# Decay-level products of a gated linear attention as 32- and 64-wide blocks: packing, small masks, and a spread by ScalarE

## The chip, the cores and the metric

The kernel runs on one core of one Trainium2 chip. The metric is the device time of one execution in microseconds (us). The kernel before takes 1532.53 us, the median of three runs (1532.47 to 1537.33).

## The reference, cut to what matters

The program is a block of two models in a row, for 256 tokens of width 1024: a first block (two gated feed-forward layers around an LRU, a local attention and a memory attention), then two layers (`LAYERS`) of a token mix and a mixture of experts. The change concerns one part of the token mix, the gated linear attention called hgrn2, with 4 heads of 128 key and 128 value features and chunks of 64 tokens:

```python
b = jnp.cumsum(gb, axis=2)
rel = b[:, :, :, None, :] - b[:, :, None, :, :]
decay = jnp.exp(jnp.where(causal, rel, -jnp.inf))
attn = jnp.einsum('bhtd,bhtsd,bhsd->bhts', qb, decay, kb)
intra = jnp.einsum('bhts,bhsv->bhtv', attn, vb)
```

Between chunks a state carries the same decay on, so that the whole is one causal attention matrix for each head whose entry (t, s) is the sum over d of q[t,d] exp(b[t,d] - b[s,d]) k[s,d].

## The kernel before, in words

The factor exp(b[t] - b[s]) can't be split into a factor of t and one of s over the whole sequence without leaving the range of float32. The kernel splits it by levels. `LEVELS` is 1, 2, 4, ..., 128. At level L the sequence is cut into pairs of blocks of L tokens. With b at the end of the left block as the origin, the right block's queries are scaled by exp(b - origin) and the left block's keys by exp(origin - b); both are written into one tile `hy` (queries in the odd blocks, keys in the even ones). The product of `hy` with itself over the 128 features then holds the attention of the pair (left keys, right queries), and also much that isn't wanted. The diagonal is a product of its own, of the plain keys `hk` and queries `hq`.

The loop `for n in range(8)` on TensorE makes product n (n = 0 the diagonal, n >= 1 the level `LEVELS[n - 1]`) for each of the two 128-token halves `t` and each of 4 heads `h`: 8 products with 128 stationary and 128 moving columns in float32, into `bank[4]` and `bank[5]` (L2055). A last product (L2067) couples the two halves. On VectorE `add_level` takes each product out of its bank: n = 0 by a multiplication with the diagonal mask (L2911), n >= 1 by a `copy_predicated` under the mask of the level, from `level_mask[:, n - 1]` (L2913); each time two instructions of 512 columns, into `attT`, which holds the transposed attention matrix. GpSimd builds `level_mask` (8 masks of 128 columns) near the start of the program (L724 to L740).

Around these products lies other work, in a fixed order for each engine. A round n is on TensorE: the projection `gates{n}` for n >= 1 (L1422: 48 instructions of 256 moving columns, whose weights have been split into two parts by ScalarE, L874, and VectorE, L2320), the product n (L2055), and one step `mla(n)` of a second attention (L1997 transposes, L2005 scores, L2037 transposes). On VectorE: `span(n + 1)` (L2884 and, for the last levels, L2888 and L2896 to L2900), `add_level(n)`, the two multiplications that write `hy` (L2932, L2933), a split of a weight tile (L2320), and from n = 4 the mask, the maxima and the scaling of the second attention (L2942, L2948, L2582, L2583, L2957, L2959). On ScalarE: `gate_out(n)` (L1249), the two exponentials of level n (L1280, L1281), a split (L874), and from n = 4 the exponentials of the second attention (L1302). Product n waits for `hy` of round n - 1; `hy` of round n waits for the exponentials of level n and stands behind `add_level(n)` on VectorE.

After the rounds come `second_pT` (L2011), the values (L2076 to L2079 and L2088, L2090), a normalisation on VectorE (L2972 to L2988, with the low part of `ymT`, L2983), the branch and output projections (L1445), and the mixture of experts.

Of the kernel before, what the change touches and what calls it, by code (L numbers as in the profile page):

```python
# [35 lines left out]
HGH, DK = 4, 128  # L36
# [4 lines left out]
CHUNK = 64  # L41
FB = 256
RING = 6
TILE = 2048
LEVELS = [1, 2, 4, 8, 16, 32, 64, 128]
NEG = -1.0e30
MISC = QL + KVL + ROPE
# [29 lines left out]
def build(nc, a):  # L77

    ctx = ExitStack()
    with ctx:  # L80
# [9 lines left out]
        x = sb("x", [P, T, D])  # L90
# [121 lines left out]
        hy = view(10240, HGH * SEQ)  # L212
        attT = view(11264, 3, HGH, P)
        p_first = view(19008, MH, P)
        p_second = view(16960, MH, SEQ)
# [198 lines left out]
        s = Signals()  # L414
# [247 lines left out]
        def _(pool):  # L662
            done = [0]

            def link(ins):
                done[0] += 1
                ins.then_inc(s["pool_chain"], 1)
                pool.wait_ge(s["pool_chain"], done[0])
# [53 lines left out]
            for p, of_count in ((1, NE - 2), (2, NE - 5), (3, n_wide), (13, NE - 4), (14, n_wide + n_half - 1), (15, NE - 3)):  # L722
                pool.memset(ranks[:, 2, p:p + 1], float(of_count))
            pool.memset(level_mask[:, 0:7, :], 0.0)  # L724
            link(pool.memset(chunk_seg[:, :], 1.0))
            pool.memset(chunk_seg[:, :].rearrange("p (m c) -> p m c", c=CHUNK)[:, :, 0:1], 0.0)
            upper = []
            for n, L in enumerate(LEVELS[:-1]):
                upper.append(level_mask[:, n, :].rearrange("p (m two c) -> p m two c", two=2, c=L)[:, :, 1, :])
                ins = pool.memset(upper[n], 1.0)  # L730
            link(ins)
            for n, L in enumerate(LEVELS[:-1]):
                ins = pool.affine_select(out=upper[n], in_=upper[n], compare_op=ALU.is_ge, fill=0.0,
                                         base=0, pattern=[[-2 * L, P // (2 * L)], [0, L]], channel_multiplier=1)
            link(ins)
            for n, L in enumerate(LEVELS[:-1]):
                pool.affine_select(out=upper[n], in_=upper[n], compare_op=ALU.is_ge, fill=0.0,
                                   base=L - 1, pattern=[[2 * L, P // (2 * L)], [0, L]], channel_multiplier=-1)
            link(pool.memset(level_mask[:, 7, :], 0.0))
            pool.affine_select(out=level_mask[:, 7, :], in_=level_mask[:, 7, :], compare_op=ALU.not_equal, fill=1.0,  # L740
                               base=0, pattern=[[-1, P]], channel_multiplier=1).then_inc(s["patterns"], 1)
            for l in range(LAYERS):

                pool.wait_ge(s["x"], 16 + 8 * l)
                pool.iota(slot_row, [[1, PICKS]], base=1, channel_multiplier=0, allow_small_or_imprecise_dtypes=True)
                pool.iota(slot_col[:, 0:1], [[0, 1]], base=0, channel_multiplier=1, allow_small_or_imprecise_dtypes=True)
                pool.memset(xg[:, :, 2 * SEQ:PICKS], 0.0)
                pool.memset(key[:, 0:1], -1.0)
                pool.memset(key[:, 1:2], -0.5)
                link(pool.memset(before, 1.0))  # L750
                pool.affine_select(out=before, in_=before, compare_op=ALU.is_ge, fill=0.0, base=-1,
                                   pattern=[[1, P]], channel_multiplier=-1).then_inc(s["slot_patterns"], 1)
# [8 lines left out]
        def _(act):  # L761
# [440 lines left out]
            for l in range(LAYERS):  # L1202
# [65 lines left out]
                for n, L in enumerate(LEVELS):  # L1268
# [13 lines left out]
                    if n < 6:  # L1282
                        split(tiles[13 + n])
                    elif n == 7:
                        split(f"br_b0.{l}", after=f"gates6.{l}")
# [66 lines left out]
        def _(pe):  # L1352
# [594 lines left out]
            for l in range(LAYERS):  # L1947
# [14 lines left out]
                by_token(f"proj5.{l}", bank[7], hT_lo_l)  # L1962
                pe.wait_ge(s["h_act"], 3 * l + 1)
                by_token(f"misc0.{l}", bank[0], hT_lo_l)
                by_token(f"misc1.{l}", bank[1], hT_lo_l)
                pe.wait_ge(s["h_act"], 3 * l + 2)
                by_token(f"misc2.{l}", bank[2], hT_lo_l)
# [8 lines left out]
                pe.wait_ge(s["cT_out"], 2 * l + 1)  # L1976
                pe.wait_ge(s["h_act"], 3 * l + 3)
                pe.wait_ge(s["h_dve"], 3 * l + 3)
# [61 lines left out]
                for n in range(8):  # L2040
                    if n >= 3:
                        pe.wait_ge(s["gates"], 8 * l + n - 2)
                    if n:
                        by_token(f"gates{n}.{l}", bank[n % 3], hT_lo_l)
                    if n == 0:
                        pe.wait_ge(s["h_dve"], 3 * l + 2)
                        pe.wait_ge(s["h_act"], 3 * l + 1)
# [15 lines left out]
                pe.wait_ge(s["hy"], 8 * l + 8)  # L2063
                pe.wait_ge(s["level_added"], 9 * l + 8)
                y = hy[:, :].rearrange("p (h s) -> p h s", h=HGH)
# [75 lines left out]
                pe.wait_ge(s["member"], 2 * run - 1)  # L2141
                pe.wait_ge(s["slot_patterns"], run)
                member = rt[:, 14, :]
# [33 lines left out]
        def _(v):  # L2177
            done = [0]

            def link(ins):  # L2180

                done[0] += 1
                ins.then_inc(s["dve_chain"], 1)
                v.wait_ge(s["dve_chain"], done[0])
# [609 lines left out]
            for l in range(LAYERS):  # L2794
# [14 lines left out]

                v.wait_ge(s["h_act"], 3 * l + 3)  # L2810
                for h in range(HGH):
# [63 lines left out]
                v.wait_ge(s["hg"], run)  # L2875
                v.wait_ge(s["h_act"], 3 * l + 1)
                g_flat = hg[:, :, :].rearrange("p h s -> p (h s)")
# [24 lines left out]

                def add_level(n, mask):

                    v.wait_ge(s["level"], 9 * l + n + 1)
                    m = level_mask[:, mask, :].unsqueeze(1).broadcast_to([P, HGH, P])
                    here = level_mask[:, mask, :].bitcast(I32).unsqueeze(1).broadcast_to([P, HGH, P])
# [12 lines left out]
                for n, L in enumerate(LEVELS):  # L2920
                    if n + 1 < len(LEVELS):
                        span(n + 1, LEVELS[n + 1])
                    if n:
                        v.wait_ge(s["level"], 9 * l + n + 1)
                        add_level(n, n - 1)
                    else:
                        add_level(0, 7)
                    v.wait_ge(s["decay"], 8 * l + n + 1)
# [62 lines left out]
                split(f"w_out0.{l}")  # L2991
                v.wait_ge(s["h_act"], 3 * l + 2)
                v.wait_ge(s["oaT"], run)
# [51 lines left out]
                v.wait_ge(s["scores"], run)  # L3045
                v.wait_ge(s["slot_patterns"], run)

# [135 lines left out]
```

## Time and profile before

| what | value |
|---|---|
| median of three runs | 1532.53 us (1532.47 to 1537.33) |
| the profiled execution | span 1534.2 us (the profile gives no other time for it) |
| TensorE busy, its share of the span | 1406.9 us, 92% |
| VectorE busy | 910.0 us, 59% |
| ScalarE busy | 646.6 us, 42% |
| GpSimd busy | 43.6 us, 3% |
| mean granted TensorE clock | 0.966 |

Busy time of an engine is the union of its instructions. The span is from the first to the last instruction of the core. The two runs of the rounds lie from 620 to 700 us (layer 0) and from 1125 to 1205 us (layer 1).

### The profile page before, as it was taken

How to read it: one execution, taken by the hardware profiler on the slowest of the kernel's cores; microseconds unless marked ns; L12 is line 12 of the kernel's file. 1: busy time of each engine (PE TensorE's matmuls, PEld its weight loads, DVE VectorE, ACT ScalarE, POOL GpSimd, SP SyncE). 2: the span in 40 equal slices, each digit the busy share in tenths (PEclk: the TensorE clock that was granted, in tenths of full speed). 3: DMA queues.
4: the chain of work that ended last, by engine and by line, in shares of the span. 5: the costliest groups of instructions: out<-in, count | busy, mean ns of one | idle time of the engine just before them, and what ended most of it. 6: DMA issues, size and time to landing. Idle time of an engine off the chain costs nothing.

```text
span 1534.2 us, 27016 instructions
## 1 busy us (share of the span) xinstructions
PE 1406.9 (92%) x10772; PEld 1135.5 (74%) x10772; DVE 910.0 (59%) x1458; ACT 646.6 (42%) x1044; POOL 43.6 (3%) x105
## 2 busy tenths in 40 slices
PE   6999999999999899998889999969999888999994
PEld 6999979669999797897645666649879764566662
DVE  5978868748788844789550443244477966054323
ACT  5444446644434543554222544234444522244322
POOL 3300000000000000000010000000000001000000
PEclk9999999999999999999889999979999998999998
DMA  9899874357999654432549999995443264999995
GB/s 321 281 337 345 317 238 147 111 187 249 331 347 334 222 153 151 131 119 86 217 183 363 417 418 418 416 335 165 141 138 110 88 242 175 362 416 419 417 417 222
DMA packets 159802, 402.09 MB, mean 262 GB/s; under 512 B 6410, under 2 KB 102396, under 8 KB 143324
## 3 DMA queue, kind: packets, MB, share of 16 engines
q1 hardware_dynamic: 158768, 398.81, 70.9%
q8 instruction: 67, 1.10, 0.3%
q10 hardware_dynamic: 380, 1.08, 0.3%
q0 software_dynamic: 560, 0.88, 0.2%
q14 instruction: 27, 0.22, 0.0%
HBM read 399.70 MB, written 1.05 MB: 261 GB/s over the span
## 4 chain that ended last, share of the span: by engine, by line
PE 74%; DVE 14%; ACT 6%; DMA 3%; issue 2%; ACTq 0%; DVEq 0%
PE bank L1553 16%; PE bank L1422 8%; PE bank L1628 8%; PE bank L1565 7%; PE bank L1445 5%; PE bank L1410 5%; PE bank L1636 5%; PE bank L1676 3%; PE bank L1471 3%; PE bank L1687 2%; PE bank L1985 1%; DVE sb_w_lo L2320 1%; DMA sb_ring<-in_w_down 1%; DMA sb_xn<-in_w_up 1%; PE bank L1601 1%
## 5 line engine op out<-in xcount | busy, mean ns | idle before, releaser
L1553 PE MATMUL bank<-sb_hT_hi,sb_w_hi 128*128 128x256 f32 x704 | 199.7, 284 | 3.1 <-DVE sb_hT_lo L2297 2.2
L1553 PE MATMUL bank<-sb_hT_lo,sb_w_hi 128*128 128x256 f32 x704 | 198.0, 281 | 0.0
L1553 PE MATMUL bank<-sb_hT_hi,sb_w_lo 128*128 128x256 f32 x704 | 197.5, 281 | 0.0
L2342 DVE TENSOR_TENSOR sb_w_lo<-sb_ring,sb_w_hi 128x1024 fp32r<-128x1024 f32 x128 | 151.2, 1223 | 64.4 <-ACT sb_w_hi L894 64.3
L894 ACT ACTIVATE sb_w_hi<-sb_ring 128x1024 fp32r<-128x1024 f32 x128 | 128.8, 1055 | 115.3 <-PE bank L1553 114.9
L2320 DVE TENSOR_TENSOR sb_w_lo<-sb_ring,sb_proj_hi 128x1024 fp32r<-128x1024 f32 x100 | 118.0, 1220 | 63.0 <-ACT sb_proj_hi L874 62.8
L1553 PEld LDWEIGHTS bank<-sb_hT_hi,sb_w_hi 128*128 128x128 f32 x704 | 133.8, 190 | 5.1 <-issue 4.3
L1553 PEld LDWEIGHTS bank<-sb_hT_lo,sb_w_hi 128*128 128x128 f32 x704 | 134.9, 192 | 0.7
L1422 PE MATMUL bank<-sb_w_lo,sb_hT_hi 128*128 128x256 f32 x480 | 134.7, 281 | 0.0
L874 ACT ACTIVATE sb_proj_hi<-sb_ring 128x1024 fp32r<-128x1024 f32 x100 | 101.0, 1064 | 78.7 <-PE bank L1410 35.1
L1553 PEld LDWEIGHTS bank<-sb_hT_hi,sb_w_lo 128*128 128x128 f32 x704 | 133.6, 190 | 0.0
L1422 PE MATMUL bank<-sb_proj_hi,sb_hT_hi 128*128 128x256 f32 x416 | 118.5, 285 | 0.8 <-DVE sb_w_lo L2320 0.8
L1422 PE MATMUL bank<-sb_proj_hi,sb_hT_lo_l 128*128 128x256 f32 x416 | 117.5, 282 | 0.0
L2372 DVE SCALAR_TENSOR_TENSOR sb_arena<-sb_arena,sb_ccol 128x1280 f32 (+1 forms) x84 | 107.6, 1281 | 0.7
L1628 PE MATMUL bank<-sb_ring,sb_arena 128*32 128x128 f32 (+1 forms) x1568 | 95.6, 312 | 2.4 <-DMA sb_ring<-in_w_gate 1.3
L2443 DVE SCALAR_TENSOR_TENSOR sb_small_a<-sb_small_a,sb_by_slot,bank 128x256 f32<-128x256 f32 (+2 forms) x32 | 15.3, 479 | 134.7 <-PE bank L1628 112.6
L1422 PEld LDWEIGHTS bank<-sb_w_lo,sb_hT_hi 128*128 128x128 f32 x480 | 90.3, 188 | 0.1
L1628 PEld LDWEIGHTS bank<-sb_ring,sb_arena 128*32 128x32 f32 (+1 forms) x1568 | 64.5, 119 | 32.4 <-issue 15.3
L1422 PEld LDWEIGHTS bank<-sb_proj_hi,sb_hT_hi 128*128 128x128 f32 x416 | 78.5, 189 | 1.4 <-DVE sb_w_lo L2320 1.3
L1422 PEld LDWEIGHTS bank<-sb_proj_hi,sb_hT_lo_l 128*128 128x128 f32 x416 | 78.2, 188 | 0.0
L1410 PE MATMUL bank<-sb_hT_hi,sb_w_lo 128*128 128x256 f32 x256 | 72.6, 284 | 0.0
L2418 DVE TENSOR_TENSOR sb_w_lo<-sb_ring,sb_moe_hi 128x1024 fp32r<-128x1024 f32 x60 | 70.2, 1220 | 2.4 <-ACT sb_moe_hi L948 2.4
(564 smaller groups left out, 2919.9 us busy)
## 6 DMA issues: line engine op xcount, KB each, us to landing
sb_ring<-in_w_in SPq DMA_DIRECT2D x46, 1024.0 KB, 5.6
sb_ring<-in_ffn_w_in SPq DMA_DIRECT2D x44, 1024.0 KB, 8.8
sb_ring<-in_w_up SPq DMA_DIRECT2D x42, 1024.0 KB, 11.7
sb_ring<-in_w_gate SPq DMA_DIRECT2D x42, 1024.0 KB, 11.5
sb_arena<-in_ada_w SPq DMA_DIRECT2D x32, 1280.0 KB, 7.3
sb_ring<-in_w_down SPq DMA_DIRECT2D x38, 1024.0 KB, 14.7
sb_ring<-in_ffn_w_out SPq DMA_DIRECT2D x22, 1024.0 KB, 8.3
sb_arena<-in_w_down SPq DMA_DIRECT2D x16, 1024.0 KB, 11.4
```

The lines of the kernel that those rows point to most:

```text
L874: A(mix_hi(name)[:, c], buffer(pos)[:, c], ACT.Copy).then_inc(s["mix_hi"], 1)
L894: A(w_hi[:, q % 2, c], ring[:, (pos0 + q) % RING, c], ACT.Copy).then_inc(s["w_hi"], 1)
L1410: ins = mm(out[:, j * SEQ:(j + 1) * SEQ], w[wp][:, k, j * P:(j + 1) * P], h_parts[hp][:, k, :], start=k == 0 and m == 0 and (turned is Non ...
L1422: ins = mm(out[:, t * FB:(t + 1) * FB], h_parts[hp][:, k, t * P:(t + 1) * P], w[wp][:, k, :], start=k == 0 and m == 0, stop=k == KC - 1 an ...
L1445: ins = mm(out[2 * t + half][:, :], l_parts[hp][:, kk, t * P:(t + 1) * P], w[wp][:, kk, half * 512:(half + 1) * 512], start=start and kk = ...
L1553: ins = mm(bank[4 + 2 * p + b][:, jj * SEQ:(jj + 1) * SEQ], w[wp][:, k, jj * P:(jj + 1) * P], h_parts[hp][:, k, :], start=k == 0 and m == ...
L1565: ins = mm(acc[2 * t + half][:, :], h, w[wp][:, kk, half * 512:(half + 1) * 512], start=start and kk == 0 and m == 0, stop=stop and kk == ...
L1628: ins = mm(out[c * m:(c + 1) * m, 0:4 * m], xw[:, 4 * kh + k, :], w[:, k, c * 4 * m:(c + 1) * 4 * m], start=kh == 0 and k == 0, stop=kh == ...
L1636: ins = mm(out[:, :], xw_parts[xp][:, 4 * kh + k, 0:P], w[wp][:, k, :], start=kh == 0 and k == 0 and m == 0, stop=kh == 1 and k == 3 and m ...
L2320: ins = tt(w_lo[:, pos % RING, c], ring[:, pos % RING, c], mix_hi(name)[:, c].bitcast(F32), ALU.subtract)
L2342: ins = tt(w_lo[:, slot, c], ring[:, slot, c], w_hi[:, q % 2, c].bitcast(F32), ALU.subtract)
L2372: ins = stt(out, w, ccol[:, k:k + 1], out, M, AD)
```

## The change

The products n = 0 to 5 (diagonal and levels 1 to 16) are made only inside blocks of 32 tokens on the diagonal of the matrix: for each half and head four products with 32 stationary and 32 moving columns, each to its own group of 32 partitions. Products 6 and 7 (levels 32 and 64) are made only for the wanted pairs: two products of 32 x 32, or one of 64 x 64. The results are packed into one bank (256 columns, 512 at n = 7), and the banks 4 and 5 alternate by n, so that a product waits for the `add_level` of two rounds before and no more for the last. `add_level` is one instruction of 256 columns under a 32-column mask for n <= 5, into a packed tile `att_diag`; two copies of 32 partitions and 256 columns for n = 6; one copy of 64 partitions and 512 columns for n = 7, these straight into `attT`. ScalarE spreads `att_diag` into `attT` by four copies (32 partitions, 256 columns) in round 6. GpSimd clears `attT` at the start of each layer, once `x` is complete, and builds the masks at the start of the program in 64 small chained instructions.

```diff
-            pool.memset(level_mask[:, 0:7, :], 0.0)
+            pool.memset(level_mask[:, :, 0:BLOCK], 0.0)
...
+            for n, L in enumerate(IN_BLOCK):
+                for g in groups:
+                    z = upper[n, g.start]
+                    link(pool.affine_select(out=z, in_=z, compare_op=ALU.is_ge, fill=0.0,
+                                            base=0, pattern=[[-2 * L, BLOCK // (2 * L)], [0, L]], channel_multiplier=1))
...
             for l in range(LAYERS):
+                pool.wait_ge(s["x"], 12 + 8 * l)
+                pool.memset(att_blocks, 0.0).then_inc(s["layer_patterns"], 1)
                 pool.wait_ge(s["x"], 16 + 8 * l)
...
                     if n < 6:
                         split(tiles[13 + n])
+                    elif n == 6:
+                        act.wait_ge(s["layer_patterns"], 2 * l + 1)
+                        act.wait_ge(s["level_added"], 9 * l + 6)
+                        for g in range(0, P, BLOCK):
+                            ins = A(att_blocks[g:g + BLOCK, :, g:g + BLOCK], att_diag[g:g + BLOCK, :, :], ACT.Copy)
+                        ins.then_inc(s["h_act"], 1)
...
-                        pe.wait_ge(s["level_added"], 9 * l + n)
+                        if n > 1:
+                            pe.wait_ge(s["level_added"], 9 * l + n - 1)
                         left = right = hy[:, :].rearrange("p (h s) -> p h s", h=HGH)
+                    if n <= len(IN_BLOCK):
+                        width, blocks = BLOCK, [(g, g) for g in range(0, P, BLOCK)]
+                    else:
+                        width = LEVELS[n - 1]
+                        blocks = [(g, g + width) for g in range(0, P, 2 * width)]
                     for t in range(T):
                         for h in range(HGH):
-                            ins = mm(bank[4 + t][:, h * P:(h + 1) * P], left[:, h, t * P:(t + 1) * P],
-                                     right[:, h, t * P:(t + 1) * P], start=True, stop=True)
+                            at = (t * HGH + h) * width
+                            for j, i in blocks:
+                                ins = mm(bank[4 + n % 2][j:j + width, at:at + width], left[:, h, t * P + j:t * P + j + width],
+                                         right[:, h, t * P + i:t * P + i + width], start=True, stop=True)
...
+                pe.wait_ge(s["h_act"], 4 * l + 4)
...
-                    for t in range(T):
-                        src = bank[4 + t][:, :].rearrange("p (h c) -> p h c", h=HGH)
-                        if n == 0:
-                            ins = tt(attT[:, t], src, m, M)
-                        else:
-                            ins = v.copy_predicated(attT[:, t], here, src)
+                    out = bank[4 + n % 2]
+                    if n <= len(IN_BLOCK):
+                        src = out[:, 0:T * HGH * BLOCK].rearrange("p (b c) -> p b c", c=BLOCK)
+                        mask = level_mask[:, n - 1 if n else 7, 0:BLOCK]
+                        if n == 0:
+                            ins = tt(att_diag, src, mask.unsqueeze(1).broadcast_to([P, T * HGH, BLOCK]), M)
+                        else:
+                            here = mask.bitcast(I32).unsqueeze(1).broadcast_to([P, T * HGH, BLOCK])
+                            ins = v.copy_predicated(att_diag, here, src)
+                    else:
+                        L = LEVELS[n - 1]
+                        src = out[:, 0:T * HGH * L].rearrange("p (b c) -> p b c", c=L)
+                        v.wait_ge(s["layer_patterns"], 2 * l + 1)
+                        for g in range(0, P, 2 * L):
+                            ins = cp(att_blocks[g:g + L, :, g + L:g + 2 * L], src[g:g + L, :, :])
...
                 v.wait_ge(s["level"], 9 * l + 9)
+                v.wait_ge(s["h_act"], 4 * l + 4)
```

The last wait is for the four copies of ScalarE, since `att_diag` lies in the third part of `attT`, which product L2067 fills. The semaphore `slot_patterns` becomes `layer_patterns` and counts two a layer; `h_act` counts four a layer and not three.

## Rows read from the trace of the kernel before

**Rows 1.** The chain of waits by time, layer 0 (start us, us, what)

```profile
625.85 5.97 PE bank L1422 x48
631.82 1.78 PE bank L2055 x16
...
656.93 1.80 PE bank L2055 x16
...
681.26 0.74 DVE sb_arena L2913
...
702.37 7.40 PE bank L1445 x24
```

**Rows 2.** By stretch: length, busy PE PEld DVE ACT POOL, PEclk, DMA share, GB/s

```profile
620.00:659.00 39.00, 36.19 (x310) 35.82 (x310) 28.23 (x33) 23.80 (x41) 0.00 (x0) 1.00 0.36 112
659.00:700.00 41.00, 37.41 (x326) 36.01 (x324) 35.70 (x66) 21.66 (x55) 0.00 (x0) 1.00 0.29 101
```

**Rows 3.** VectorE in order of time, rounds 4 to 7 of layer 0

```profile
658.82 1.35 DVE L2913 COPY_PREDICATED sb_arena<-sb_level_mask,bank 128x512 f32<-128x512 int32 x2 [2.27 <-PE bank L2055]
...
679.42 0.42 DVE L2897 TENSOR_TENSOR sb_arena<-sb_arena 128x256 f32<-128x256 f32 x1
679.75 0.42 DVE L2898 TENSOR_TENSOR sb_arena<-sb_arena 128x256 f32<-128x256 f32 x1
...
680.62 1.36 DVE L2913 COPY_PREDICATED sb_arena<-sb_level_mask,bank 128x512 f32<-128x512 int32 x2
...
689.71 0.69 DVE L2932 TENSOR_TENSOR sb_arena<-sb_arena 128x512 f32<-128x512 f32 x1 [1.19 <-ACT sb_arena L1281]
```

**Rows 4.** ScalarE in order of time, round 6 of layer 0

```profile
680.52 0.61 ACT L1281 ACTIVATE sb_arena<-sb_arena 128x512 f32<-128x512 f32 x1
686.01 0.51 ACT L1302 ACTIVATE sb_arena<-sb_arena,sb_stat 128x256 f32<-128x256 f32 x1 [4.87 <-DVE sb_stat L2583]
```

**Rows 5.** A group of TensorE by line and shape: xrecords, busy us, mean ns

```profile
L1628 PE MATMUL bank<-sb_ring,sb_arena 128*32 128x128 f32 x1024 | 30.8, 274 | 1.3 <-DMA sb_ring<-in_w_gate 1.3
```

**Rows 6.** TensorE in order of time, around L2122 of layer 0

```profile
744.99 0.62 PE L1445 MATMUL bank<-sb_w_lo,sb_hT_hi 128*128 128x512 f32 x2
745.45 0.62 PE L1445 MATMUL bank<-sb_tail_hi,sb_hT_lo_l 128*128 128x512 f32 x2
746.00 0.67 PE L2122 MATMUL bank<-sb_modc,sb_ident 128*32 128x4 f32 x32
746.59 1.13 PE L1825 MATMUL bank<-sb_arena,sb_ones 128*128 128x512 f32 x2
```

**Rows 7.** TensorE in order of time, product 8 to the branch product, layer 0

```profile
691.06 1.16 PE L2067 MATMUL bank<-sb_arena 128*128 128x128 f32 x8 [2.26 <-DVE sb_arena L2933]
...
696.22 0.43 PE L2088 MATMUL bank<-sb_small_a,sb_arena 128*64 128x128 f32 x2
...
698.68 0.66 PE L2090 MATMUL bank<-sb_arena 128*64 128x128 f32 x6
702.37 0.73 PE L1445 MATMUL bank<-sb_proj_hi,sb_ymT_hi 128*128 128x512 f32 x2 [3.04 <-DVE sb_ymT_lo L2983]
```

**Rows 8.** GpSimd in order of time, the masks

```profile
41.28 0.88 POOL L724 MEMSET sb_level_mask<- 128x896 f32 x1
...
43.87 5.28 POOL L733 TENSOR_SCALAR_AFFINE_SELECT sb_level_mask<-sb_level_mask 128x64 f32<-128x64 f32 x7
```

**Rows 9.** VectorE in order of time, start of the program and of layer 0

```profile
43.96 0.59 DVE L2206 TENSOR_SCALAR sb_stat<-sb_stat 128x2 f32<-128x2 f32 x1
...
518.11 0.15 DVE L2228 TENSOR_SCALAR sb_stat<-sb_stat 128x1 f32<-128x1 f32 x1
...
518.50 0.49 DVE L2233 TENSOR_SCALAR sb_xn<-sb_x,sb_stat 128x512 f32<-128x512 f32 x1
```

**Rows 10.** TensorE alone by stretch: length, busy, PEclk, DMA share, GB/s

```profile
704.00:706.00 2.00, 2.00 (x7) 0.50 0.00 0
```

**Rows 11.** The chain of waits by time, the same branch product of layer 1

```profile
1207.50 5.83 PE bank L1445 x24
```

More of the change, by code:

```diff
@@ L45 @@
 LEVELS = [1, 2, 4, 8, 16, 32, 64, 128]
+BLOCK = 32
+IN_BLOCK = [L for L in LEVELS if 2 * L <= BLOCK]
 NEG = -1.0e30
@@ L213, in build @@
         attT = view(11264, 3, HGH, P)
+        att_diag = view(12288, T * HGH, BLOCK)
+        att_blocks = attT[:, 0:T].rearrange("p t h c -> p (t h) c")
         p_first = view(19008, MH, P)
@@ L723, in _ @@
                 pool.memset(ranks[:, 2, p:p + 1], float(of_count))
-            pool.memset(level_mask[:, 0:7, :], 0.0)
+            pool.memset(level_mask[:, :, 0:BLOCK], 0.0)
             link(pool.memset(chunk_seg[:, :], 1.0))
[L726 to L738, printed above, removed]
@@ L739, in _ @@
-            link(pool.memset(level_mask[:, 7, :], 0.0))
-            pool.affine_select(out=level_mask[:, 7, :], in_=level_mask[:, 7, :], compare_op=ALU.not_equal, fill=1.0,
-                               base=0, pattern=[[-1, P]], channel_multiplier=1).then_inc(s["patterns"], 1)
+            link(pool.memset(chunk_seg[:, :].rearrange("p (m c) -> p m c", c=CHUNK)[:, :, 0:1], 0.0))
+            groups = [slice(g, g + BLOCK) for g in range(0, P, BLOCK)]
+            upper = {}
+            for n, L in enumerate(IN_BLOCK):
+                for g in groups:
+                    upper[n, g.start] = level_mask[g, n, 0:BLOCK].rearrange("p (m two c) -> p m two c", two=2, c=L)[:, :, 1, :]
+                    link(pool.memset(upper[n, g.start], 1.0))
@@ new lines, in _ @@
+            for n, L in enumerate(IN_BLOCK):
+                for g in groups:
+                    z = upper[n, g.start]
+                    link(pool.affine_select(out=z, in_=z, compare_op=ALU.is_ge, fill=0.0,
+                                            base=0, pattern=[[-2 * L, BLOCK // (2 * L)], [0, L]], channel_multiplier=1))
+            for n, L in enumerate(IN_BLOCK):
+                for g in groups:
+                    z = upper[n, g.start]
+                    link(pool.affine_select(out=z, in_=z, compare_op=ALU.is_ge, fill=0.0,
+                                            base=L - 1, pattern=[[2 * L, BLOCK // (2 * L)], [0, L]], channel_multiplier=-1))
@@ L742, in _ @@
+            for g in groups:
+                z = level_mask[g, 7, 0:BLOCK]
+                link(pool.affine_select(out=z, in_=z, compare_op=ALU.not_equal, fill=1.0,
+                                        base=0, pattern=[[-1, BLOCK]], channel_multiplier=1))
+            pool.sem_inc(s["patterns"], 1)
             for l in range(LAYERS):
+                pool.wait_ge(s["x"], 12 + 8 * l)
+                pool.memset(att_blocks, 0.0).then_inc(s["layer_patterns"], 1)
                 pool.wait_ge(s["x"], 16 + 8 * l)
@@ L751, in _ @@
                 pool.affine_select(out=before, in_=before, compare_op=ALU.is_ge, fill=0.0, base=-1,
-                                   pattern=[[1, P]], channel_multiplier=-1).then_inc(s["slot_patterns"], 1)
+                                   pattern=[[1, P]], channel_multiplier=-1).then_inc(s["layer_patterns"], 1)
                 pool.wait_ge(s["xn_hi"], l + 1)
@@ L1962, in _ @@
                 by_token(f"proj5.{l}", bank[7], hT_lo_l)
-                pe.wait_ge(s["h_act"], 3 * l + 1)
+                pe.wait_ge(s["h_act"], 4 * l + 1)
                 by_token(f"misc0.{l}", bank[0], hT_lo_l)
                 by_token(f"misc1.{l}", bank[1], hT_lo_l)
-                pe.wait_ge(s["h_act"], 3 * l + 2)
+                pe.wait_ge(s["h_act"], 4 * l + 2)
                 by_token(f"misc2.{l}", bank[2], hT_lo_l)
@@ L1976, in _ @@
                 pe.wait_ge(s["cT_out"], 2 * l + 1)
-                pe.wait_ge(s["h_act"], 3 * l + 3)
+                pe.wait_ge(s["h_act"], 4 * l + 3)
                 pe.wait_ge(s["h_dve"], 3 * l + 3)
@@ L2046, in _ @@
                         pe.wait_ge(s["h_dve"], 3 * l + 2)
-                        pe.wait_ge(s["h_act"], 3 * l + 1)
+                        pe.wait_ge(s["h_act"], 4 * l + 1)
                         left, right = hk, hq
@@ L2063, in _ @@
                 pe.wait_ge(s["hy"], 8 * l + 8)
-                pe.wait_ge(s["level_added"], 9 * l + 8)
+                pe.wait_ge(s["level_added"], 9 * l + 7)
                 y = hy[:, :].rearrange("p (h s) -> p h s", h=HGH)
@@ L2141, in _ @@
                 pe.wait_ge(s["member"], 2 * run - 1)
-                pe.wait_ge(s["slot_patterns"], run)
+                pe.wait_ge(s["layer_patterns"], 2 * run)
                 member = rt[:, 14, :]
@@ L2808, in _ @@
                         modulation(1)
-                v.wait_ge(s["h_act"], 3 * l + 3)
+                v.wait_ge(s["h_act"], 4 * l + 3)
                 for h in range(HGH):
@@ L2875, in _ @@
                 v.wait_ge(s["hg"], run)
-                v.wait_ge(s["h_act"], 3 * l + 1)
+                v.wait_ge(s["h_act"], 4 * l + 1)
                 g_flat = hg[:, :, :].rearrange("p h s -> p (h s)")
@@ L2922, in _ @@
                         span(n + 1, LEVELS[n + 1])
-                    if n:
-                        v.wait_ge(s["level"], 9 * l + n + 1)
-                        add_level(n, n - 1)
-                    else:
-                        add_level(0, 7)
+                    add_level(n)
                     v.wait_ge(s["decay"], 8 * l + n + 1)
@@ L2991, in _ @@
                 split(f"w_out0.{l}")
-                v.wait_ge(s["h_act"], 3 * l + 2)
+                v.wait_ge(s["h_act"], 4 * l + 2)
                 v.wait_ge(s["oaT"], run)
@@ L3045, in _ @@
                 v.wait_ge(s["scores"], run)
-                v.wait_ge(s["slot_patterns"], run)
+                v.wait_ge(s["layer_patterns"], 2 * run)
                 def r(n):
```

4 lines of the change are left out of this document (1 added, 3 removed).

## The prediction

> **What bounds the kernel now.** I read the chain of waits first, because the shares of busy time are averages. In rounds 1 to 4 of layer 0 the chain is TensorE alone: 48 gate records, the 16 of the level product, 8 transposes, and again; from product 1 at 631.82 to product 4 at 656.93 are three rounds of 8.37 us with nothing between their pieces [rows 1]. TensorE is busy 36.19 of 39 us there, VectorE only 28.23 [rows 2]. So there every microsecond of the level product is on the path, and VectorE's copy of a product is not. After product 4 the chain crosses over: VectorE takes the product out, writes `hy`, splits a tile and makes the maxima, ScalarE makes exponentials, VectorE goes on to the second copy on the chain (round 6), and so on until the branch products at 702.37 [rows 1]. In this second stretch TensorE is still busy 37.41 of 41 us [rows 2]; its rows follow each other with next to no gap until 2.26 us before product 8 [rows 7], so VectorE can gain only if TensorE gets shorter too. It does, in the same change.
>
> **TensorE, the level product.** Before: 8 products are 16 records, 1.78 us, so 0.112 us a record [rows 1]. After, for n = 0 to 5: 32 products, 64 records of 32 stationary and 32 moving columns. The trace has no such record, so I bound it. From below: L2122 has 32 stationary columns, the four groups of partitions in turn, and 4 moving columns; 32 records take from 746.00 to 746.59, 18.4 ns each [rows 6]. From above: L1628 has the same stationary width and 128 moving columns, 30.8 us for 1024 records, 30.1 ns each [rows 5]. That is a quarter of the 112 ns of a 128-wide record with as many moving columns, so the four groups do run beside each other. 32 moving columns lie on the line between the two at 18.4 + 28/124 x 11.7 = 21.0 ns, and 64 records are 1.35 us. I add 0.09 us for changing over from full-width work: pairs of L1445 start 0.46 us apart (744.99, 745.45), so the next would start at 745.91, and L2122 starts 0.09 later; L1825 behind it shows no such gap [rows 6]. Product: 1.44 us, between 1.18 and 2.02 (64 x 30.1 ns + 0.09). Against 1.79 before, the gain in rounds 1 to 4 is 4 x 0.35 = 1.40 us a layer (from 2.4 down to -0.9). Product 0 is hidden, since TensorE then waits for the split of the first gate tile. Products 5 to 7 fall by 0.3, about 1.0 and about 0.9 us; they gain nothing themselves, but leave TensorE the room for what VectorE gains.
>
> The Trainium skill ("TensorEngine Tiling (Array Packing)", section "Instruction Overhead") speaks against this edit: a matmul with one moving column takes as long as one with 60, and one shouldn't tile a dimension that is already small. Its 60 cycles at 2.4 GHz would be 25 ns, and with 25 ns a record the product would be an estimated 1.6 us and not 1.35. The trace's 18.4 ns for four columns is already under that figure. The same page ("Key Properties") says that a change of tiling mode drains the engine; the 0.09 us above agrees with it.
>
> **VectorE, the copies.** Before: two of 512 columns, 1.36 us. After, for n <= 5: one of 256. A 256-column instruction shows 0.42 us and the next starts after 0.33 [rows 3]. I take 0.46 for a predicated one. Gain 0.90 us, on the chain only in round 4. In rounds 1 to 3 TensorE covers it (VectorE sat idle 2.27 us before its copy in round 4 [rows 3]), and in round 5 VectorE waits for ScalarE's exponentials afterwards. Round 6: two copies, 0.42 + 0.33 = 0.75, gain 0.61 us, on the chain. Round 7: the copy lies in front of a wait of 1.19 us for ScalarE [rows 3], gain 0. Sum 1.51 us a layer (1.4 to 1.7).
>
> **ScalarE, the spread.** Four copies of 256 columns, at 0.3 to 0.5 us by the exponential of that width [rows 4], together 1.2 to 2.0 us. They stand behind the exponentials of level 6, and the engine is idle 4.87 us there before it gets the next maxima [rows 4]. The gains of this chain move both ends nearly alike and leave some 4 us. Cost 0; if that cover were gone, 1.2 to 2.0 us a layer. TensorE's new wait for them stands behind product 8, and VectorE's in front of its last copy, both some 8 us later.
>
> **The alternating banks** take a wait away that never ended last: in each round `hy` is written behind `add_level` on the same engine. Gain 0.
>
> **GpSimd.** The clearing of `attT` is 1024 columns, 0.88 x 1024/896 = 1.0 us [rows 8]. It starts when the last quarter of `x` is written, just when VectorE makes the root and the scaling that TensorE waits for. VectorE's small TENSOR_SCALAR takes 0.15 us alone and 0.59 us while GpSimd builds masks [rows 8, 9], so the two do disturb each other. The instructions at risk are L2228 and L2233 [rows 9]. Cost 0.4 us a layer, between 0 and 1.0. The masks themselves: before, selects of 0.75 us on average (5.28/7, rows 8) lie beside a normalisation on VectorE that is on the chain; after, short memsets lie there first and selects of a quarter of the columns. I take a gain of 0.3 us once, between -1 and +1. Later ones, to about 65 us, lie beside work in which TensorE is the bound.
>
> **The sum.** A layer: 1.40 + 1.51 + 0 - 0.4 = 2.51 us; two layers 5.0; with 0.3 at the start 5.3 us. The profiled execution's 1534.2 us become 1528.9. It stands 1.7 us above the median of the runs, 1532.53, and I carry the difference to the median: **1527.2 us**. 0.3% is 4.6 us, about what a measurement of this kernel can tell from no change; so this is just on the far side of it. Everything after the rounds depends on them through the residual `x`, and the expert weights are loaded into a ring that is freed by work behind the rounds, so I let the gain carry through in full.
>
> **Rivals.**
>
> *The products don't shorten.* At 30.1 ns a record, as L1628, the product is 2.02 us, and rounds 1 to 4 lose 0.9 us a layer. Left: -0.9 + 1.5 - 0.4 = 0.2 a layer, 0.7 us in all: 1531.8. For it: nothing shows 32 moving columns. Against: the moving columns are a quarter.
>
> *The groups don't overlap (slower).* The nearest rows that show a narrow product without fourfold overlap are the values, 64 wide: 42 records from 696.22 to 698.68, 58.6 ns each [rows 7]. With that, 64 records and the changeover are 3.84 us; rounds 1 to 4 cost 4 x 2.05 = 8.2 us more and product 0 about 1 us, against 1.1 gained: 8.1 us a layer, 16.2 in all, less 0.3: 1548.4. It decides from 31 ns a record, where 4 x (64r + 0.09 - 1.79) passes 1.1. Against: L2122 and L1628 both show four groups at 18 and 30 ns.
>
> *The clock.* The branch products of 24 records take 7.40 us in layer 0 and 5.83 in layer 1 [rows 1, 11], since the granted clock went from 1.00 (2.4 GHz) to 0.50 (1.2 GHz) at 704 after TensorE had stood still for 3.04 us [rows 7, 10]; in layer 1 the same gap did not bring it down. The same two outcomes may come the other way round: 1.6 us a site either way, and there are a few sites. A drop more in layer 1 and at one other place gives 1527.2 + 3.2 = 1530.4; the drop of layer 0 gone as well as one other, 1524.0. TensorE's gap before product 8 grows by about half a microsecond, which speaks a little for the former.
>
> *The products at the floor.* At 18.4 ns without a changeover the product is 1.18, rounds 1 to 4 gain 2.4 a layer and the whole 7.4 us: 1525.1.
>
> **How the numbers follow.** The forecast as summed (1525.5 to 1529): 0.44. Products at the floor or a clock drop gone (1522 to 1525.5): 0.17. Products don't shorten: 0.14. A clock drop more, or GpSimd at its upper price: 0.17. Groups don't overlap or some other loss over 0.3%: 0.08. The range 1522 to 1532 leaves the last case out and some of the edges. Faster by over 0.3% (below 1527.9) is two thirds of the first case and the second with a little of the rest, since a clock drop gone can make up for dearer products: 0.53. Within 0.3%: 0.38. Slower: 0.09.
>
> **What would show it.** The product's 64 records in 1.3 to 1.5 us and the chain of rounds 1 to 4 at about 8.02 us a round, and not 8.37; one 256-column copy at 0.46; round 6 on VectorE 0.6 shorter; ScalarE's four copies inside its idle time; VectorE's L2228 or L2233 of each layer longer beside the memset. The forecast fails if a record takes over 30 ns, if the chain turns to ScalarE in round 6, if TensorE becomes the bound in rounds 5 to 7 so that VectorE only waits longer, or if the clock falls at other places.

## The result, and the profile after

The changed kernel takes 1520.59 us, the median of six runs (1517.69 to 1523.65); the kernel before, run beside it, 1532.5. The ratio is 0.9921, with a 95% interval from 0.9905 to 0.9937. Run again later it came at 0.994 (0.9922 to 0.9958), 1521.34 against 1530.86 us. So the change gives 9 to 12 us, 0.6 to 0.8%. I had forecast 5.3 us, and a range that ended at 1522.0: right in sign, and less than half of the 11.9 us of the first measurement. One run of all that follow is left out of its median: the kernel of experiment 8 once took 1996.93 us at a mean granted clock of 0.65, and its other three runs 1514.23 to 1517.91.

The chain of waits of the changed kernel, layer 0, by time (a record is one matmul instruction in the trace; a float32 product of 32 columns makes two):

```profile
621.71 5.97 PE bank L1440 x48
627.68 0.69 PE bank L2081 x50
628.38 1.01 PE bank L2015 x8
629.38 5.71 PE bank L1440 x48
635.09 0.69 PE bank L2081 x50
...
644.20 5.72 PE bank L1440 x48
...
650.43 0.62 ACT sb_arena L1292
651.06 0.53 ACT sb_arena L1293
651.67 0.69 DVE sb_arena L2962
...
672.10 0.41 DVE sb_arena L2947
672.52 0.43 DVE sb_arena L2947
...
682.13 2.08 PE bank L2093 x8
684.20 1.40 PE bank L2029 x8
...
694.34 7.40 PE bank L1463 x24
```

Against [rows 1], the gate products take the same 5.71 us, and the level product (L2081, 64 records, of which this view counts 50) 0.69 us and not 1.78. The transposes behind it went from 0.87 to 1.01. Together that is 0.83 us on the chain, of which 0.14 are the changeover between narrow and full-width work as this view shows it. A round holds the same other work and takes 7.41 us (627.68 to 635.09), not 8.37. The chain cuts its pieces at modelled ends; where the changeover lies is seen from the starts:

```profile
627.40 0.28 PE L1440 MATMUL bank<-sb_proj_hi,sb_hT_lo_l 128*128 128x256 f32 x1
627.61 0.76 PE L2081 MATMUL bank<-sb_arena 128*32 128x32 f32 x64
628.31 1.08 PE L2015 MATMUL bank<-sb_ident,sb_arena 128*96 128x128 f32 x8
```

The gate records ahead of it start 0.12 us apart, and the product starts 0.21 after the last of them. So 0.09 us lie ahead of the product, as I had forecast, and some 0.05 behind it. In round 4 the chain no longer goes through the product at all, but through ScalarE's exponentials.

VectorE and ScalarE of the changed kernel in order of time:

```profile
650.64 0.44 DVE L2941 COPY_PREDICATED sb_arena<-sb_level_mask,bank 128x256 f32<-128x256 int32 x1 [1.66 <-PE bank L2081]
651.67 0.69 DVE L2962 TENSOR_TENSOR sb_arena<-sb_arena 128x512 f32<-128x512 f32 x1 [0.60 <-ACT sb_arena L1293]
...
672.10 0.84 DVE L2947 COPY sb_arena<-bank 32x256 f32<-32x256 f32 x2
```

```profile
672.51 1.68 ACT L1300 ACTIVATE sb_arena<-sb_arena 32x256 f32<-32x256 f32 x4
677.08 0.51 ACT L1320 ACTIVATE sb_arena<-sb_arena,sb_stat 128x256 f32<-128x256 f32 x1 [2.89 <-DVE sb_stat L2610]
```

The copy is 0.44 us (0.46 forecast) and the two of round 6 are 0.84 (0.75). But in round 4 VectorE then waits 0.60 us for ScalarE, so only part of that gain arrives. ScalarE's four copies take 1.68 us and still leave it idle for 2.89 us.

The clock of the changed kernel by stretch (TensorE alone; length, busy, clock, DMA share, GB/s):

```profile
678.00:680.00 2.00, 1.70 (x16) 1.00 0.80 272
680.00:682.00 2.00, 0.00 (x0) 0.93 0.55 223
682.00:684.00 2.00, 1.87 (x9) 0.50 0.00 0
684.00:686.00 2.00, 2.00 (x15) 0.72 0.00 0
```

TensorE stands still for 2.42 us ahead of product 8, where it was 2.26 [rows 7], and then works at 0.50 (1.2 GHz): product 8 takes 2.08 us, and 1.16 before. So here some time was lost that my sum did not hold. How often this happens is counted where the prediction is gone through.

The same VectorE instructions in both traces bound the stretches. From the start of the scan of `cum` to the start of the scaling of the attention's output, the rounds take 80.22 and 80.20 us before (layers 0 and 1), 76.35 and 76.48 after. Where no clock falls in them, as in several of the traces below, they take 75.43. So the rounds give 4.8 us a layer by their own work, of which the clock took about 1 back here.

### The profile page after: what moved, and what is told of

It is laid out like the page before. It is cut to its first block, busy times and chain, and to the rows that moved or that the text cites. A ratio compares the mean times of both kernels' runs of the same rounds, so it can differ in the third digit from the quotient of the medians.

```text
span 1518.6 us, 28267 instructions
## 1 busy us (share of the span) xinstructions
PE 1386.7 (91%) x11380; PEld 1118.5 (74%) x11380; DVE 895.2 (59%) x1444; ACT 649.3 (43%) x1052; POOL 63.0 (4%) x148
## 3 DMA queue, kind: packets, MB, share of 16 engines
q8 instruction: 71, 1.16, 0.3%
## 4 chain that ended last, share of the span: by engine, by line
PE 74%; DVE 13%; ACT 6%; DMA 4%; issue 2%; ACTq 0%; DVEq 0%; SPq 0%
PE bank L1571 16%; PE bank L1440 8%; PE bank L1646 7%; PE bank L1583 7%; PE bank L1428 6%; PE bank L1463 5%; PE bank L1654 5%; PE bank L1694 3%; PE bank L1489 3%; PE bank L1705 2%; DMA sb_ring<-in_w_down 1%; DVE sb_w_lo L2347 1%; DMA sb_xn<-in_w_up 1%; PE bank L1619 1%; PE bank L2003 1%
```

## The experiments

**1. TensorE's part alone, on the kernel before.**

```diff
-                            ins = mm(bank[4 + t][:, h * P:(h + 1) * P], left[:, h, t * P:(t + 1) * P],
-                                     right[:, h, t * P:(t + 1) * P], start=True, stop=True)
+                            for j, i in blocks:
+                                ins = mm(bank[4 + t][j:j + width, h * P + i:h * P + i + width],
+                                         left[:, h, t * P + j:t * P + j + width],
+                                         right[:, h, t * P + i:t * P + i + width], start=True, stop=True)
```

> The kernel before with TensorE's part alone: the narrow products, each written to its place in the two old banks; masks, VectorE's copies of 512 columns, waits and the start of the program as before. Theory (the narrow product costs 0.69 us and 0.14 of changeover, against 1.79): rounds 1 to 4 take 7.41 us each and not 8.37, 3.8 us a layer, and the time is about 1532.5 - 7.7 = 1524.8 us, with 3 us either way for the clock. Rival (VectorE's shorter copies carry the gain, as my sum had it for more than half): rounds 1 to 4 are about 0.35 us shorter each and the time is about 1529.7. Second rival (the start and the clock made the gain): no change, 1532.

Measured: 1526.21 us, ratio 0.9955 (0.9938 to 0.9973), so 6.9 us faster. The chain of layer 0:

```profile
622.51 5.97 PE bank L1422 x48
628.48 0.69 PE bank L2061 x50
629.17 1.01 PE bank L1997 x8
630.18 5.71 PE bank L1422 x48
635.88 0.69 PE bank L2061 x50
...
651.50 1.36 DVE sb_arena L2920 x2
```

A round is 7.40 us with VectorE's copies as long as they were. The stretch of the rounds is 76.25 us in layer 0, 3.97 shorter than before, and no clock falls in it (layer 1 takes 77.88, with a fall at product 8); the whole change reaches 75.43. So of the 4.8 us the products give 4.0 and everything else, the copies above all, 0.8. This is the reverse of my sum, which had 1.40 and 1.51.

**2. The 32-wide products twice.**

```diff
-                            for j, i in blocks:
+                            for j, i in (blocks + blocks if n <= len(IN_BLOCK) else blocks):
```

> The changed kernel with each 32-wide product of n = 0 to 5 issued twice (128 records, the same results), so that a product costs near the 1.44 us of my prediction. Theory: a product takes 1.38 us, rounds 1 to 4 are 0.69 us longer each, 2.8 a layer, and the time is 1520.6 + 5.5 = 1526.1 us. Rival (the product has left the path that sets the end): within 1 us of 1520.6.

Measured: 1524.93 us, ratio 0.9958 (0.9941 to 0.9974), some 4 us above the changed kernel. The chain:

```profile
627.23 1.23 PE bank L2081 x82
628.45 1.01 PE bank L2015 x8
```

64 records more cost 0.54 us, 8.4 ns each, and not the 0.69 that I expected. So the first 64 are 0.54 us too, with 0.15 of fixed cost around them. The product is on the path in rounds 1 to 3: 3 x 0.54 = 1.6 us a layer. In round 4 the longer product takes up the 0.60 us for which VectorE waited for ScalarE, and costs next to nothing. The stretch of the rounds is 77.89 and 78.52 us against 76.35 and 76.48, all four with a fall of the clock in them, so 1.5 and 2.0 us longer. By the ratios, 0.9958 against 0.9921 and 0.994, it is 3 to 6 us in all, and the 3.2 of both layers lie in that.

With the changeover behind it this product costs 1.37 us, nearly the 1.44 of my prediction. Its ratio makes 1526.1 us of the 1532.5 of the first measurement, near the 1527.2 that I forecast.

**3. The same records in another order.** The changed kernel with the loop over the groups of partitions outside:

```diff
-                    for t in range(T):
-                        for h in range(HGH):
-                            at = (t * HGH + h) * width
-                            for j, i in blocks:
+                    for j, i in blocks:
+                        for t in range(T):
+                            for h in range(HGH):
+                                at = (t * HGH + h) * width
```

> The changed kernel with the order of the products turned: all halves and heads of one group of 32 output partitions, then the next group (n = 7 is as it was). Theory (the record is cheap because four groups run beside each other): neighbours share a group, a record costs about 27 ns, a product 1.7 us, rounds 1 to 4 are 1.0 us longer each, and the time is 1520.6 + 8 = 1528.7 us. Rival (a 32-wide record is that cheap in any order): 0.69 us a product and 1520.6.

Measured: 1529.96 us, ratio 0.9984 (0.9968 to 1.0).

```profile
626.06 1.84 PE bank L2081 x64
627.90 1.01 PE bank L2015 x8
```

1.84 us for the same 64 records, 28.7 ns each with the fixed cost and an estimated 26 without its 0.15 us: no less than the 1.78 us of the full-width product. Layer 0, in which no clock falls, takes 79.47 us and not 75.43. The whole gain of the narrow product is that four groups run beside each other, and in these kernels it is there only if neighbours in the program belong to different groups.

**4. Why my floor was no floor.** L2122 of the kernel before (L2149 after) gave 18.4 ns for 4 moving columns; the level products with 32 run at 8.4. Two more sets of 32 records stand ahead of it here and are overwritten by it:

```diff
+                        for k in range(4):
+                            for g in range(4):
+                                mm(bank[6][32 * g:32 * g + 32, 4 * k:4 * k + 4], ident[:, 32 * k:32 * k + 32], modc[:, l, 24 + 4 * g:28 + 4 * g],
+                                   start=True, stop=True)
+                        for k in range(4):
+                            for g in range(4):
+                                mm(bank[6][32 * g:32 * g + 32, 32 * k:32 * k + 32], ident[:, k::4], modc[:, l, 0:32],
+                                   start=True, stop=True)
```

> The changed kernel with two more sets of 16 products ahead of the 16 small ones of L2149 (32 records at 18.4 ns, my floor), which then overwrite them: first 32 stationary columns next to each other and 4 moving columns next to each other; second the stationary columns with the stride of 4 as before and 32 moving columns next to each other. Theory (the floor was set by the stationary columns with their stride): the first set runs at 8 to 11 ns a record as the level products do, the second at 18. Rival (by the number of moving columns, some floor per instruction at 4 columns): the first set too runs at 18 ns.

TensorE in order of time:

```profile
733.97 0.44 PE L2149 MATMUL bank<-sb_modc,sb_ident 128*32 128x4 f32 x32
734.24 0.69 PE L2153 MATMUL bank<-sb_modc,sb_ident 128*32 128x32 f32 x32
734.73 0.66 PE L2157 MATMUL bank<-sb_modc,sb_ident 128*32 128x4 f32 x32
735.32 1.98 PE L1843 MATMUL bank<-sb_arena,sb_ones 128*128 128x512 f32 x4
```

From start to start: 0.27 us with both operands contiguous (8.4 ns a record), 0.49 with stationary columns four apart and 32 contiguous moving ones (15.3; I had expected 18), 0.59 with 4 moving columns that are four apart as well (18.4). At 8.4 ns it makes no difference whether 4 columns move or 32: the second set differs from the level products in shape and order by the stride of its stationary columns alone. It is one run with one trace (1520.3 us); layer 1 of it shows 0.27, 0.48 and 0.60 us.

**5. The masks at the start of the program.** The kernel before with one line ahead of the masks:

```diff
+            pool.wait_ge(s["x"], 1)
             pool.memset(level_mask[:, 0:7, :], 0.0)
```

> The kernel before with the level masks built only after the first quarter of x is final (some 200 us) and not at 41 us. Theory (GpSimd's long selects hold up VectorE's small instructions in the normalisation at 41 to 46 us, and the change freed 1.9 us there): the gate product after it starts near 46.9 and not 48.8 us, time 1532.5 - 1.9 = 1530.6. Rival (it came from elsewhere, such as the first loads or the clock): it still starts at 48.8, no change.

Measured: 1530.36 us, ratio 0.9991 (0.9971 to 1.0011), which by itself says nothing. VectorE's rows say more; here with the masks late:

```profile
40.33 1.22 DVE L2245 CUSTOM_DVE_ANT_0 sb_arena<-sb_arena 128x1024 f32<-128x1024 f32 x1
...
42.73 0.17 DVE L2200 TENSOR_SCALAR sb_stat<-sb_stat 128x2 f32<-128x2 f32 x1
...
43.79 0.17 DVE L2207 TENSOR_SCALAR sb_stat<-sb_stat 128x2 f32<-128x2 f32 x1
...
45.52 2.35 DVE L2343 TENSOR_TENSOR sb_w_lo<-sb_ring,sb_w_hi 128x1024 fp32r<-128x1024 f32 x2
```

And in the kernel before, where the row with 0.59 us stands in [rows 9]:

```profile
40.13 1.22 DVE L2244 CUSTOM_DVE_ANT_0 sb_arena<-sb_arena 128x1024 f32<-128x1024 f32 x1
...
42.54 0.53 DVE L2199 TENSOR_SCALAR sb_stat<-sb_stat 128x2 f32<-128x2 f32 x1
...
46.23 2.42 DVE L2342 TENSOR_TENSOR sb_w_lo<-sb_ring,sb_w_hi 128x1024 fp32r<-128x1024 f32 x2
```

The stretch takes 5.19 us with the masks late, 6.10 before, and 5.25 in the changed kernel (39.10 to 44.35). So the masks are worth 0.9 us. Not all of it is the selects': the row with 0.53 us, which takes 0.17 with the masks late, lies beside a memset that runs ahead of them on GpSimd:

```profile
42.06 0.98 POOL L725 MEMSET sb_chunk_seg<- 128x1024 uint8 x1
```

Of the 1.88 us by which the changed kernel's trace is ahead at the end of the stretch, the other 1.03 lie before it: it begins at 39.10, 40.13 and 40.33 in the three traces, and the program is the same up to it, so no run ties it to the change. My 1.9 us in the expectation took all of it for the masks'.

**6. One more copy on VectorE.** The changed kernel with

```diff
                     out = bank[4 + n % 2]
+                    cp(view(13824, 512), out[:, :])
```

> The changed kernel with one more copy of 512 columns (0.61 us more on VectorE) ahead of every add_level, which nobody reads. Theory (VectorE's copy is on the path in round 6 alone: before round 4's hy VectorE waits 0.60 us for ScalarE, in round 5 3.29, in round 7 1.88): 0.6 us a layer, 1521.9 us. Rival (my sum: the copies of rounds 4 and 6 are on the path): 1.2 us a layer, 1523.0. Second rival (all of rounds 1 to 7 count): over 4 us a layer.

Measured: 1523.85 us, ratio 0.9954 (0.9937 to 0.9971); the changed kernel beside it had 1521.34. In layer 0, where no clock falls in the rounds, they take 76.07 us against 75.43: 0.64 us, one copy of the eight. That is the theory's 0.6, and not 1.2. In layer 1 two falls of the clock cover it (79.14), so the difference of the medians, 2.5 us, is not all the copies'.

**7. The changed kernel once more.** No edit.

> The changed kernel once more, unaltered, for more runs beside the kernel before and a second trace. Theory: of the 11.9 us, the rounds give 3.8 us a layer, the masks 0.9 us once, and 3 to 4 us are the clock, which falls at other places from one execution to the next: the ratio comes again near 0.992, and in the trace the stretch from the last quarter of x to the scan of layer 0 takes 97.9 us (clock stays up at q_up) or 100.0 us (it falls). Rival (the clock's part is chance of one trace and the first six runs): the ratio is nearer 0.9945, which is what 7.6 + 0.9 us make.

Measured: 1521.34 us, ratio 0.994 (0.9922 to 0.9958). It lies nearer to the rival, 0.9945, than to the theory, and its interval holds both. In this trace the rounds take 75.44 us in layer 0 and 78.56 in layer 1, where the clock falls twice: in the first gate product (8.06 us in place of 5.97) and at product 8. q_up (L2003, the products of the latents, ahead of the rounds) takes 9.70 and 9.41 us in the two layers. The same program has 8.01 twice in its other trace. So the clock's falls differ from one execution to the next, and are worth an estimated 3 us either way in a single time (78.56 against 75.44 in these two layers).

**8. TensorE kept at work in two gaps.** The changed kernel with products that nobody reads, ahead of product 8 and of the branch product:

```diff
                 second_pT(0, P_BANK)
+                pe.wait_ge(s["level_added"], 9 * l + 7)
+                for _ in range(2):
+                    mm(bank[4][:, :], ones[:, :], x[:, 0, 0:512], start=True, stop=True)
                 pe.wait_ge(s["hy"], 8 * l + 8)
-                pe.wait_ge(s["level_added"], 9 * l + 7)
...
                 ins.then_inc(s["mla_pv"], 1)
+                for _ in range(3):
+                    mm(bank[6][:, :], ones[:, :], x[:, 0, 0:512], start=True, stop=True)
```

> The changed kernel with TensorE kept at work in two of its gaps, by products that nobody reads: two of 512 columns before product 8 (0.85 us each, gap 2.42 us), three before the branch product (gap 3.04 us). Theory (the shorter products lengthen the gap, the clock falls at product 8 in both layers, 2.08 us in place of 1.1, and again at the branch products, 7.4 in place of 5.83): 0.9 + 1.6 us a layer come back, 5.0 in all, 1520.6 - 5.0 = 1515.6 us. Rival (the clock falls somewhere else as soon as it is held here, or the fillers delay what they precede): within 1.5 us of the changed kernel.

Measured: 1514.24 us, the median of three runs, ratio 0.9902 (0.9875 to 0.9928). TensorE in order of time:

```profile
677.95 1.88 PE L2091 MATMUL bank<-sb_x,sb_ones 128*128 128x512 f32 x4
680.54 1.16 PE L2095 MATMUL bank<-sb_arena 128*128 128x128 f32 x8 [0.71 <-DVE sb_arena L2967]
```

And its chain of waits:

```profile
682.00 1.11 PE bank L2029 x8
...
691.85 5.83 PE bank L1463 x24
```

The gap is 0.71 us and not 2.42, the transposes behind product 8 take 1.11 and not 1.40, the branch product 5.83 and not 7.40. The rounds take 75.43 and 75.42 us. Then the same kernel again:

> The changed kernel with fillers before product 8 and before the branch product, unaltered once more, for an interval beside the next kernel. Theory (the clock's falls in these two places are made by the gaps): from the scan to the normalisation 75.4 us in both layers, ratio near 0.990. Rival (it was chance of four runs): near 0.9935, as the changed kernel.

Measured: 1516.93 us, ratio 0.9898 (0.9875 to 0.9921), the rounds 75.43 and 75.44. Four layers of four have no fall in these two places. By the ratios (0.9902 and 0.9898 against 0.9921 and 0.994) the two places cost the changed kernel 3 to 6 us, some of it (the branch product of [rows 1]) there before the change.

**9. And in a third gap**, behind the transposes of the latents, where TensorE waits 2.02 us for ScalarE:

```diff
                 ins.then_inc(s["cT"], 1)
+                pe.wait_ge(s["h_dve"], 3 * l + 3)
+                for _ in range(2):
+                    mm(bank[7][:, :], ones[:, :], x[:, 0, 0:512], start=True, stop=True)
```

> The same with two fillers more, behind the transposes of the latents, where TensorE waits 2.02 us for ScalarE ahead of q_up. Theory: q_up takes 8.0 us in every layer of every run; of the kernels with narrow products most had that already in their traces, one had 9.7 in one layer, so 0.5 to 2 us are left to gain: 1515 us. Rival (the fillers delay q_up, or the clock falls later instead): no gain over the kernel with two places.

Measured: 1514.36 us, ratio 0.9889 (0.9869 to 0.991), q_up 8.01 us in both layers. By its ratio this is the fastest of all kernels, 1.1% under the kernel before; over the one with two places its gain, 1 to 2 us, is within the intervals.

**10. The same third gap in the kernel before.** A first try had five fillers in front of the transposes as well:

```diff
+                pe.wait_ge(s["h_dve"], 3 * l + 3)
+                for _ in range(5):
+                    mm(bank[7][:, :], ones[:, :], x[:, 0, 0:512], start=True, stop=True)
                 pe.wait_ge(s["latents"], run)
```

> The kernel before with TensorE kept at work ahead of the q_up products by products of 512 columns that nobody reads: five before the transposes of the latents, two behind them. Theory (in the traces of the kernel before the clock falls here in both layers, q_up takes 11.0 us and not 8.0, and this is 2 to 3 us a layer of what the changed kernel gained without touching it): 1532.6 - 5.5 = 1527.1 us, q_up 8.0 us. Rival (the fall was chance of that trace; most runs of the kernel before don't have it): less than 2 us.

Measured: 1540.18 us, ratio 1.0055 (1.0035 to 1.0075), slower. I had misread the gap: TensorE waits 0.68 us in front of the transposes, and 4.29 us of fillers held them up. Its q_up is 8.01 us. Then with the two fillers behind alone:

> The kernel before with two fillers behind the transposes of the latents, and none in front, where five of them held TensorE up. Theory (the clock's fall at q_up, 11.0 us in place of 8.0 in both layers of three traces with wide products, is a real part of the time before): 1532 - 5 = 1527 us. Rival (the fall is in few runs): 1531 to 1532.

Measured: 1528.99 us, ratio 0.9977 (0.9964 to 0.999): 3.5 us of the kernel before (1.5 to 5.5) come back with the clock at q_up, where I had expected 5. Its chain, layer 1:

```profile
1101.03 8.01 PE bank L1988 x24
```

and that of the kernel before:

```profile
1107.38 11.03 PE bank L1985 x24
```

## Why the prediction was wrong, step by step

**The bound was read rightly.** TensorE alone in rounds 1 to 4, the cross-over to VectorE and ScalarE after them, product 0 and the split hidden: as predicted, and shown by experiments 1, 2 and 6. Only the place of the cross-over moved: it now comes ahead of product 4 and not behind it, by ScalarE.

**The term that failed is the level product: 1.44 us predicted, 0.69 + 0.14 measured.** I took 18.4 ns a record as the floor from L2122 [rows 6] and went up from there to 21.0. The record costs 8.4 ns (experiment 2). L2122 was dear for another reason than its shape: its stationary columns, and its moving ones too, lie four elements apart (experiment 4). So even my "products at the floor", 1.18 us, was too dear, and the range built on it ended at 1522. Per layer the term is 3.98 us by the chain of layer 0 (three rounds of 0.96 and 1.10 of product 4) and 3.97 by experiment 1, not 1.40. This is 5.1 us in all, most of the miss of 6.6; the smaller misses below partly cancel.

That four groups run beside each other I had read rightly from L1628 [rows 5], and experiment 3 shows it; the rival that they don't falls. The overhead of some 60 cycles for each matmul that the Trainium skill states ("TensorEngine Tiling (Array Packing)", section "Instruction Overhead"), an estimated 25 ns at 2.4 GHz, does not show between groups: 64 records of 32 columns start 8.4 ns apart on average. With one group at a time the 26 to 28.7 ns of experiment 3 are near it.

**VectorE's copies: 1.51 us predicted, 0.8 measured.** The copies themselves were sized well (0.44 for 0.46, 0.84 for 0.75). But only half of the gain of round 4 arrives, 0.41 of 0.90 us (from product 1 to `hy` of round 4 the chain takes 24.40 us in experiment 1 and 23.99 here), and 0.53 of 0.61 in round 6: in round 4 ScalarE's exponentials of level 4 stand behind `gate_out(4)` on its queue, which waits for the gate product, and VectorE waits 0.60 us for them. I had looked at what was in front of the copy and not at what `hy` waits for besides.

**GpSimd: a loss of 0.4 us a layer predicted, next to none found.** In layer 0 the clearing runs from 515.65 for 0.96 us, right beside L2228 and L2233 of [rows 9], and they take 0.15 and 0.48 us as before. In layer 1 the second takes 0.55 us and not 0.49. So this memset of float32 costs VectorE at most 0.06 us, where the selects at 44 us and the memset of bytes ahead of them (experiment 5) each cost one small instruction some 0.4. Why is open: the small instructions have two columns there and one here, and the memsets differ in type. The masks gave 0.9 us and not 0.3 (experiment 5).

**ScalarE's spread and the banks** cost and gave nothing, as predicted: 2.89 us of idle time are left behind the four copies.

**The sum with the measured terms** is 2 x 4.8 + 0.9 = 10.5 us. The two ratios make 9 to 12.

**The clock** was a rival of mine with a chance of 0.17, for more falls. It did both. In the first trace product 8 falls in both layers (about 1 us each), where the trace of before has no such fall, and the branch product takes 7.40 and 7.39 us and not 7.40 and 5.83. Over all traces without fillers at these places product 8 is slow in 8 layers of 14 with narrow products and in 1 of 8 with wide ones; the branch product in 8 of 14 and 7 of 8. The gap ahead of product 8 alone does not decide it: with the products twice it is 2.44 us, as here, and product 8 takes 1.16 us in both layers. That the narrow products bring the fall is so not shown. At q_up the traces of kernels with wide products show 11.0 us in four layers of four (before, and with late masks), those with narrow ones and no filler at this place 8.0 in 11 layers of 18. By experiment 10 this would be worth up to an estimated 3.5 us to the change. Why the first layer's q_up, which comes ahead of any narrow product, should differ, is open: chance in few traces can't be excluded, and nothing here settles it.

## What to carry to other kernels

A bound from the nearest row holds only if the row is like the new work in everything that costs: compare strides and order, and not only the shapes. Products with few output rows pay on TensorE only when neighbours in the program belong to different groups of 32 partitions; the same 64 instructions took 0.69 or 1.84 us. And when TensorE is made faster beside work of other engines, look at its gaps: two or three products that nobody reads in each of two gaps gave back 3 to 6 us here, as long as they were shorter than the gap. The same holds for the copies: when the engine that was waited for gets faster, the next one (here ScalarE, 0.60 us) takes over.

## What the runs showed of the hardware

- Records of 32 stationary and 32 moving float32 columns in four alternating groups start 8.4 ns apart on average, those with 4 moving columns no sooner; with one group after the other it is 26 to 28.7 ns.
- Stationary columns that lie four elements apart make it 15.3 ns, and with 4 moving ones four apart too it is 18.4.
- GpSimd's selects and VectorE's work slow each other down: seven selects of 64 columns took 5.28 us beside VectorE's work at 44 us [rows 8], and 2.26 us in experiment 5, where they run at 207 us and VectorE stands idle; VectorE's instruction of two columns 0.59 and 0.17. Beside a memset of 1024 byte columns such an instruction took 0.53 us; beside one of 1024 float32 columns an instruction of one column kept its 0.15.
